# The values' projection of a sparse-attention layer moved behind compression and gates, with the first scores between its units

## The reference, cut to what matters

```python
q, k_c, v_c, k_s, v_s, k_w, v_w, gate = jnp.split(h @ w_in, split_at, axis=-1)   # 1024, 6 x 256, 48
gate = jax.nn.sigmoid(gate)
blocks = kv(t)[:, cidx] + pe                # 31 overlapping blocks of 32 tokens
kc = silu(blocks_k @ w1[0]) @ w2[0]         # compressed keys;  vc: the same of v_c
o_c = softmax(q kc^T - slope * dist) vc     # compressed branch
o_s = softmax(q k_s^T - slope * dist) v_s   # selected branch (here every block is selected)
o_w = softmax(q k_w^T - slope * dist) v_w   # window branch (the window holds all 512 tokens)
return (gate0 * o_c + gate1 * o_s + gate2 * o_w) @ w_out
```

## Time and profile before

| what | value |
|---|---|
| median of 3 runs | 2295.69 us (2295.18 to 2296.01) |
| profiled execution | 2294.17 us |
| its span, first to last instruction | 2292.9 us |
| TensorE busy | 2247.9 us, 98% of the span |
| VectorE, ScalarE, GpSimd busy | 72%, 46%, 28% |
| mean granted clock of TensorE | 0.998 |
| SyncE's queue, share of the 16 DMA engines | 30.3% |

### The profile page before, as it was taken

One profiled execution on the slowest core, in us unless ns is written; L12 is line 12 of the kernel. 1 busy time (PEld: TensorE's weight loads), 2 busy tenths in 40 slices (PEclk: granted clock), 3 DMA queues, 4 the chain that ended last, 5 costly groups with the idle time before them and its releaser, 6 DMA issues.

```text
span 2292.9 us, 34766 instructions
## 1 busy us (share of the span) xinstructions
PE 2247.9 (98%) x14151; PEld 1946.4 (85%) x14151; DVE 1641.1 (72%) x2120; ACT 1050.3 (46%) x1515; POOL 634.3 (28%) x557
## 2 busy tenths in 40 slices
PE   7999999999999999999999999999999999999999
PEld 5888778999887867778999888999887868899987
DVE  6668657889785456637888567989456984788844
ACT  4322534555334457734555346444345363544432
POOL 0110223332122048703332011332011870233200
PEclk9999999999999999999999999999999999999999
DMA  9654156775763210026774536775232202787322
GB/s 333 191 166 139 47 174 165 189 178 121 267 211 103 81 57 1 1 69 174 183 190 112 166 97 170 183 178 123 96 102 92 83 29 78 189 192 173 105 92 83
DMA packets 224373, 308.69 MB, mean 135 GB/s; under 512 B 14345, under 2 KB 165446, under 8 KB 223958
## 3 DMA queue, kind: packets, MB, share of 16 engines
q1 hardware_dynamic: 173268, 223.99, 30.3%
q0 software_dynamic: 50640, 82.29, 17.5%
q10 hardware_dynamic: 306, 0.19, 0.0%
HBM read 302.23 MB, written 4.19 MB: 134 GB/s over the span
## 4 chain that ended last, share of the span: by engine, by line
PE 84%; DVE 10%; ACT 2%; POOL 2%; issue 1%; DMA 1%; ACTq 0%; SPq 0%; DVEq 0%
PE ps L732 41%; PE ps L1180 10%; PE ps L1182 10%; PE ps L1181 10%; PE ps L879 4%; DVE w_lo L2315 2%; DVE dsa_mask L3116 1%; PE ps L1306 1%; POOL nsa_p L3487 1%; PE ps L1322 1%; DVE small L3114 1%; PE ps L928 1%; DVE h_lo L2412 1%; ACT w_hi L1631 1%; PE ps L1295 1%
## 5 line engine op out<-in xcount | busy, mean ns | idle before, releaser
L2315 DVE TENSOR_TENSOR w_lo<-w_raw,w_hi 128x1024 fp32r<-128x1024 f32 (+1 forms) x466 | 652.3, 1401 | 480.8 <-ACT w_hi L1631 479.1
L1631 ACT ACTIVATE w_hi<-w_raw 128x1024 fp32r<-128x1024 f32 (+1 forms) x472 | 495.7, 1051 | 996.7 <-PE ps L732 579.3
L1180 PE MATMUL ps<-feat_t,w_hi 128*128 128x256 f32 x1152 | 326.5, 283 | 3.1 <-DVE hid L2819 2.3
L1181 PE MATMUL ps<-feat_t,w_hi 128*128 128x256 f32 x1152 | 326.0, 283 | 0.0
L1182 PE MATMUL ps<-feat_t,w_lo 128*128 128x256 f32 x1152 | 326.0, 283 | 0.0
L3340 POOL TENSOR_TENSOR w_raw<-w_raw,w_raw 128x1024 f32<-128x1024 f32 x72 | 177.7, 2468 | 453.9 <-DVE w_lo L2315 453.9
L732 PE MATMUL ps<-h_hi,w_hi 128*128 128x512 f32 (+1 forms) x712 | 279.9, 393 | 4.8 <-DVE w_lo L2315 3.1
L732 PE MATMUL ps<-h_hi,w_lo 128*128 128x512 f32 (+1 forms) x712 | 277.2, 389 | 0.0
L732 PE MATMUL ps<-h_lo,w_hi 128*128 128x512 f32 (+1 forms) x712 | 277.2, 389 | 0.0
L1180 PE MATMUL ps<-h_hi,w_hi 128*128 128x256 f32 x864 | 244.9, 283 | 1.9 <-DVE w_lo L2315 1.9
L1181 PE MATMUL ps<-h_lo,w_hi 128*128 128x256 f32 x864 | 244.5, 283 | 0.0
(11 more groups left out here) (459 smaller groups left out, 4205.8 us busy)
## 6 DMA issues: line engine op xcount, KB each, us to landing
w_raw<-in_ffn_w_up SPq DMA_DIRECT2D x126, 512.0 KB, 6.5
w_raw<-in_ffn_w_down SPq DMA_DIRECT2D x176, 256.0 KB, 3.3
w_raw<-in_ffn_w_up POOLq DMA_DIRECT2D x72, 512.0 KB, 7.7
m_raw<-in_ada_w POOLq DMA_DIRECT2D x56, 512.0 KB, 4.8
w_raw<-in_ffn_w_gate SPq DMA_DIRECT2D x54, 512.0 KB, 5.8
w_raw<-in_hg_w_in SPq DMA_DIRECT2D x64, 256.0 KB, 3.2
w_raw<-in_ffn_w_up SPq DMA_DIRECT2D x48, 256.0 KB, 3.1
w_raw<-in_nsa_w_in SPq DMA_DIRECT2D x40, 256.0 KB, 2.9
```

The source lines that it names most:

```text
L1180: K.nc.tensor.matmul(out, hi[:, w], m_hi, start=opens and kt == f == 0, stop=False, skip_group_check=True)
L1181: K.nc.tensor.matmul(out, hi[:, w], m_lo, start=False, stop=False, skip_group_check=True)
L1631: K.nc.scalar.activation(K.half(K.hi(u), width), K.half(K.raw(u), width), ACT.Copy) \
L2315: K.nc.vector.tensor_tensor(K.half(K.lo(u), width), K.half(K.raw(u), width), hi, ALU.subtract) \
```

## The change

The values' projection (group 4) comes last. Its loads and units are listed behind the gates'. TensorE's order becomes: groups 0, 1, 2, 3; both parts of `hidden` (now in bank 0); the four gate units (now in bank 2); then a wait for the last evacuation of group 3, since the values now go to banks 4 to 7; then the four units of the values with other work between them. ScalarE and VectorE keep group 3's evacuations one by one between the splits, now the splits of the gate units and of the first two value units. The calls of `tensor_stay_busy` in the mix go, except those in other stages. The wait for all of `key_twice` becomes one per unit. `kc` moves to another place in SBUF.

```diff
-        for gi, pieces in enumerate((... k_tiles(w, slice(512, 1024)), strided(0), strided(256), k_tiles(w, slice(2560, 2608)))):
+        for gi, pieces in (... (3, strided(0)), (5, k_tiles(w, slice(2560, 2608))), (4, strided(256))):
@@ tensor_nsa_in
-            nsa_evac(K, pe, 3)
+            nsa_evac(K, pe, 2)
-    for gi in range(5):
+    for gi in range(4):
...
+    for u in range(2):
+        hidden(u)
     u0 = K.unit["nsa", 5]
-    nsa_evac(K, pe, 3)
     for u in range(4):
         pe.wait_ge(*K["w_low"].at(u0 + u))
         tensor_unit_products(K, None, u0 + u, gate_items(K, (u0 + u, u)))
-        if u < 2:
-            hidden(u)
+    nsa_evac(K, pe, 3)
+FIRST_UNITS = 3
@@ tensor_nsa_mix
-    nsa_evac(K, pe, 2)
-    nsa_evac(K, pe, 4)
-    pe.wait_ge(*K["key_twice"].at((3, 1, 1)))
-    for n in range(UNITS + 3):
+    u0 = K.unit["nsa", 4]
+    def values_in(u):
+        pe.wait_ge(*K["w_low"].at(u0 + u))
+        items = token_items(K, (u0 + u, u), range(4, 8), 512, by_bank=u == 3)
+        tensor_unit_products(K, ("nsa_in", "v"), u0 + u, items, (lambda n: None) if u == 3 else None)
+    values_in(0)
+    turn_gates()
+    pe.wait_ge(*K["c_hidden_out"].at(0))
+    scores(0)
+    values_in(1)
+    compressed_keys()
+    scores(1)
+    values_in(2)
+    scores(2)
+    values_in(3)
+    for n in range(2, UNITS + 3):
...
+        if FIRST_UNITS <= n < UNITS:
+            scores(n)
+        if n == 2:
+            nsa_evac(K, pe, 4)
+            compressed(0, 0)
...
-        if n == 0:
-            tensor_stay_busy(K, 4, 6)
-            turn_gates()
-        if n == 2:
-            tensor_stay_busy(K, 1, 4)
...
-        elif n == 4 or n == 5:
-            kept(n - 3, 4)
-            tensor_stay_busy(K, 3 if n == 4 else 2, 4)
...
+        if n == 2:
+            compressed(0, 1)
@@ scalar_nsa_in (vector_nsa_in in the same way)
-    for gi in range(6):
+    for gi in (0, 1, 2, 3, 5):
         u0 = K.unit["nsa", gi]
         for u in range(4):
-            if 0 < gi < 5:
-                evac(gi - 1, u)
+            if gi:
+                evac(3 if gi == 5 else gi - 1, u)
             scalar_split(K, u0 + u + 2)
+            if (gi, u) == (5, 1):
+                act.wait_ge(*K["c_hidden_bias"].at(0))
+                nc.scalar.activation(K.c_sig[:, :, 0:31], ..., ACT.Sigmoid, ...).then_inc(*K["c_gate"].up(0))
@@ scalar_nsa_mix
+    scalar_split(K, u0 + 2)
+    gates()
+    for n in range(FIRST_UNITS):
+        for t in (3, 2, 0, 1):
+            weights(n, t)
+        if n < 2:
+            scalar_split(K, u0 + n + 3)
+        if n == 0: ...
+    value_tile(0)
+    value_tile(2)
+    scalar_split(K, u0 + 5)
+    compressed(0, 0)
+    for n in range(FIRST_UNITS, UNITS + 4):
@@ vector_nsa_in
+            if (gi, u) == (5, 0): ...
+            elif (gi, u) == (5, 2): ...
@@ vector_nsa_mix
+    vector_split(K, u0 + 2)
+    for n in range(FIRST_UNITS):
+        for t in (3, 2, 0, 1):
+            scores(n, t)
+        reciprocal(n)
+        if n < 2:
+            vector_split(K, u0 + n + 3)
+        if n == 0:
+            for j in range(4):
+                compressed_value(j)
+    value_tile(1)
+    value_tile(3)
+    vector_split(K, u0 + 5)
+    for n in range(2, UNITS + 4):
```

More of the change, by code:

```diff
@@ L1286, in tensor_nsa_mix, with scores @@
     nc, pe = K.nc, K.pe
-    def scores(u, slot):
+    def scores(u):
         i, head, br = unit_of(u)
[L1290 to L1297, removed]
+        at = i + 4 * br
+        pe.wait_ge(*K["key_twice"].at((at // 2, at % 2, 1)))
+        for slot in range(3):
+            if u:
+                pe.wait_ge(*K["nsa_max"].at((u - 1, SLOTS[slot][-1])))
+            for t in SLOTS[slot]:
+                w, tok = (t + 1) * P, slice(t * P, (t + 1) * P)
+                out = K.ps[:, score_bank(t), IN_SLOT[t]:IN_SLOT[t] + w]
+                nc.tensor.matmul(out, K.nq[:, head, tok], K.nk[:, at, 0:w], start=True, stop=False)
+                nc.tensor.matmul(out, K.nq[:, head, tok], K.nk_lo[:, at, 0:w], start=False, stop=True) \
+                    .then_inc(*K["nsa_scores"].up((u, t)))
     def turn(u, bank):
@@ L1344, in compressed_keys @@
         pe.wait_ge(*K["c_zero_vec"].at(0))
+        pe.wait_ge(*K["c_exp"].at("gates"))
         for rows in (slice(0, 64), slice(64, P)):
-            ins = nc.tensor.matmul(K.ps[rows, 6, 0:128], K.w2[0:64, :], hs[0:64, :, :], start=True, stop=True)
+            ins = nc.tensor.matmul(K.ps[rows, OUT_BANK, 0:128], K.w2[0:64, :], hs[0:64, :, :], start=True, stop=True)
         for j in range(4):
             for gr in range(4):
-                ins = nc.tensor.matmul(K.ps[32 * j:32 * j + 31, 6, 128 + gr * 64:192 + gr * 64], hs[64:P, gr, 0:31],
+                ins = nc.tensor.matmul(K.ps[32 * j:32 * j + 31, OUT_BANK, 128 + gr * 64:192 + gr * 64], hs[64:P, gr, 0:31],
                                        K.w2[64:P, :], start=True, stop=True)
@@ L1402, in tensor_nsa_mix @@
                 turn(n - 2, bank)
-        if n % 2 and n < UNITS:
+        if n == 2:
+            compressed(0, 1)
+        elif n % 2 and n < UNITS:
             compressed((n - 1) // 8, (n - 1) % 8)
@@ L2117, in keep, with value_tile @@
         keep_turned(u, 6)
-    for n in range(UNITS + 4):
+    def value_tile(t):
+        act.wait_ge(*K["feature_sum"].at((("nsa_in", "v"), t)))
+        nc.scalar.activation(K.nv[:, t, :], K.ps[:, 4 + t, :], ACT.Copy).then_inc(*K["act_evac"].up(("nsa", 4, t)))
+    u0 = K.unit["nsa", 4]
+    scalar_split(K, u0 + 2)
[6 more added lines that the diff above has]
+        if n == 0:
+            act.wait_ge(*K["c_value"].at(0))
+            nc.scalar.activation(K.kc[:, :, :], K.ps[:, OUT_BANK, 0:128].rearrange("p (a b) -> p a b", a=4), ACT.Copy) \
+                .then_inc(*K["c_key_high"].up(0))
+    value_tile(0)
[3 more added lines that the diff above has]
+    for n in range(FIRST_UNITS, UNITS + 4):
         if n >= 7 and n % 4 == 3:
@@ L2130, in scalar_nsa_mix @@
             keep(n - 2)
-        if 1 <= n < UNITS and (n - 1) % 8 == 5:
+        if n < UNITS and (n - 1) % 8 == 5:
             compressed((n - 1) // 8, 5)
@@ L2135, in scalar_nsa_mix @@
                 weights(n, t)
[L2136 to L2140, removed]
+        if n < UNITS and (n - 1) % 8 != 5:
             compressed((n - 1) // 8, (n - 1) % 8)
@@ L3069, in vector_nsa_mix @@
             keep_turned(n - 3)
-        if n < UNITS:
+        if FIRST_UNITS <= n < UNITS:
             scores(n, 3)
-        if 1 <= n <= UNITS:
+        if FIRST_UNITS < n <= UNITS:
             reciprocal(n - 1)
-        if n < UNITS:
+        if FIRST_UNITS <= n < UNITS:
             for t in (2, 0, 1):
                 scores(n, t)
[L3077 to L3081, removed]
+        if n < UNITS:
             compressed((n - 1) // 8, (n - 1) % 8)
```

74 lines of the change are left out of this document (31 added, 43 removed).

## The result

The changed kernel takes 2299.28 us (median of 16 runs, 2297.47 to 2302.77), the kernel before 2294.81 us (16 runs, 2291.65 to 2299.01) in the same comparison: a ratio of 1.0022, 95% interval 1.0016 to 1.0029. That is 4.5 us, 0.2%, slower, and the interval reaches from 3.7 to 6.7 us. The forecast was 4.3 us more.

The account below looks back on a forecast made before the run. GpSimd's chain was taken to bound the mix's start, TensorE what follows. The subtraction 2.6 us later plus 1.7 us of clock made +4.3 us on 2295.69, so 2300.0 us; range 2293.9 to 2302.5.

Parts of the forecast that it names:

- The one number to compute: Start of GpSimd's subtraction at the mix's start: 2.6 us later before the clock; the 11.2 us behind it stay the same.
- The gates' wait: In the gate units, TensorE waits 0.7 us for unit 3's split, which is late behind evacuations of group 3.
- The new wait: Ahead of the values, TensorE stands idle 4.3 us until the last bank of group 3 is evacuated.
- The clock: Behind the new idle stretch the clock falls, adding 1.7 us; bounds nothing and twice as much.
- rival (b): A second or longer fall of the clock, in the values or at the mix's start: 2301.7, up to 2302.5 us; chance 0.22.
- (a): The forecast itself, with one fall of the clock: 2300.0 us, 0.19% more; chance 0.40.
- The copy of the last values' bank: Ahead of the compressed scores, TensorE waits for VectorE's copy: 0.65 us and two hand-overs, listed as 1.0 us.
- The constants and idle stretches at the mix's start, taken at nothing: Removing 2.6 us of constants' matmuls gains nothing there; idle 1.9 and 1.4 us ahead of two scales cost nothing, 1.7 for the range.
- Rival (d): Group 3's banks are drained in time, so the idle 4.3 us and the clock's fall go: 2294.0 us; chance 0.13.
- Rival (e): GpSimd's chain does not set the mix's start's pace; with (d), -5.1 us: 2290.6 us, 0.22% faster; chance 0.06.
- The table load's cost: On ScalarE before the sigmoid: taken as 1.28 us; with the skill's drain 2.66 us, making the idle time 5.7 us.

Follow-up runs that it names:

- the fill: The changed kernel with nine matmuls of constants put into TensorE's idle stretch ahead of the values: 2296.04 us, ratio 1.0008 to the kernel before.
- Drain first: The changed kernel, but ScalarE and VectorE empty all four banks of group 3 ahead of gate unit 2's split: 2292.73 us, ratio 0.9993 to the kernel before.
- the constants back: The changed kernel with the stay-busy matmuls at n = 4 and n = 5 put back: 2299.68 us, ratio 1.0020 to the kernel before.
- all biases late: The changed kernel, but GpSimd makes all three later compressed biases behind scale 6 of each eight units: 2305.68 us, ratio 1.0043 to the kernel before.
- the two runs on the constants: Stay-busy matmuls at n = 4 and 5 put back in the changed kernel (ratio 1.0020), and taken out of the kernel before (1.0001).
- first bias late: The changed kernel, but GpSimd makes only the first later compressed bias behind scale 5: 2296.51 us, ratio 1.0012 to the kernel before.
- its two variants: The kernel before without constants at n = 4 and 5: 2294.85 us, 1.0001; the same with the first compressed bias behind scale 5: 2292.62 us, 0.9988.
- the kernel with the drain, `hidden` and the first bias changed: The changed kernel with group 3 emptied first, halves of `hidden` between gate units, first compressed bias behind scale 5: 2292.07 us, ratio 0.9991.
- the fastest one among them: The changed kernel with `hidden` interleaved, first compressed bias late, and group 3's banks emptied two, one, one between splits: 2289.30 us, ratio 0.9979.

## Why the prediction was right

The sum was +4.3 us and the range 2293.9 to 2302.5; measured were +4.5 us (16 runs) and +4.12 us between the marks of the two traces. Point by point:

- *The one number to compute.* That only the start of GpSimd's subtraction counts held: 11.23 us from there to unit 3's transposes in both kernels, and one bias less in GpSimd's chain shortened this to 8.9 and the whole by 0.1%. One reading of the kernel before was incomplete. VectorE's maximum ends there at 845.63, but GpSimd is busy with a scale until the subtraction starts at 845.75, so its own work held the subtraction as much as the maximum did; after the change it had been idle for 10.62 us and only the maximum released it. The row of the kernel before:

```profile
843.40 2.38 POOL L3487 TENSOR_SCALAR nsa_p<-nsa_p,nsa_stat,nsa_gate 128x512 f32<-128x512 f32 x4 [1.07 <-DVE nsa_stat L3023]
```

- *The gates' wait*: 0.7 forecast, 0.54 measured.
- *The new wait*: 4.3 forecast, 4.14 measured; the values started 19.25 us behind group 3 and not 19.8. The split behind the first gate unit began 0.2 us earlier than forecast, and from it to the end of the drain it took 8.9 us (806.39 to 815.31) and not 9.2. What came behind made up for it: from the values' start to the subtraction the forecast had 33.2 us at full clock, and the two kernels with the drain or the fill took 33.5. That these two errors cancel was luck. "Drain first" showed that this wait is the drain.
- *The clock*: +1.7 forecast. The fill isolates it at 1.62 us in the traced execution. The ground for the term was thin, one fall behind 2.01 us of idle time, and behind the same 2.01 us the clock held in the changed kernel's trace; behind the 4.1 us it fell in all four traces that have this stretch. The changed kernel's traced execution is the fastest of the sixteen (2297.47 us). The mean granted clock over the sixteen was 0.9962, over the 81 executions of the kernel before that were timed beside the experiments 0.9976; over 2296 us of span this is about 3.3 us, an estimate (each clock is recorded to 0.001). So in the usual execution the clock probably cost more than 1.7 us, and rival (b), a longer fall, was not told apart from (a): the traces with the constants back and with all biases late, which have the same idle stretch, show a longer one. The drain and the fill also gained more in the times (6.7 and 3.2 us by the ratios) than in the traces (4.9 and 1.6).
- *The copy of the last values' bank*: 0.7 in the forecast's timetable and 1.0 in its list of differences, 0.83 measured.
- *The constants and idle stretches at the mix's start, taken at nothing*: confirmed by putting them back and by taking them out, 1.0020 and 1.0001. The clock did not fall there in the traces without the constants, though the stretch of 1.8 us lies close to the 2.01 us of the earlier trace rows; rival (b)'s second fall was not seen in the changed kernel's trace.
- *Rival (d)*, the drain in time, was wrong for the changed kernel, and "drain first" is what it described: forecast 1.7 us faster than before, 0.8 us in the trace. Of the 0.9 us between, 0.5 lie ahead of the values (15.99 us instead of 15.5): the split of their first unit, which (d) had left uncounted, takes 1.58 us of waiting, and the wait in the gates and the earlier start give back some of it. The rest lies between the values and the subtraction.
- *Rival (e)* fell with the two runs on the constants.

The table load's cost, where a page of the Trainium skill ("ScalarE: Activation LUTs", "What ACT_TABLE_LOAD costs") counts a drain of 1.38 us more, is settled by the trace after: the split ahead of the load ends at 808.19, the load takes 1.28 us from 808.22, and the sigmoid starts at 809.51. This trace does not agree with the page's drain.

What stays open is what the clock costs in the usual execution. Only one execution of each kernel has a trace, and the times of one kernel spread over some 3 to 8 us.

## What to carry to other kernels

Before moving a stage behind another, list what the old order covered: here the long projection hid the emptying of four banks, and the short units that took its place could not. Emptying that stands in an engine's program between the splits of the next units runs at the pace of those splits, so it starts when the units do; write it ahead of them if the next user of the banks is near. Matmuls that do nothing, placed where TensorE waited for another engine, cost nothing here, and where the clock held without them their removal gave nothing; in the stretch of 4.1 us, behind which the clock fell, they gave 1.6 us back. So do not count their removal as a gain; shorten the other engine's chain instead, at a place where that engine is idle, and check one cycle later.

## What the runs showed of the hardware

One fall of the clock had no fixed price. Between the values' first matmul and the subtraction, the same work took 33.5 us in the kernels whose clock held (33.53 with the drain first, 33.56 with the fill), 35.18 and 35.17 in two with the fall (the changed kernel and the first bias late), and 35.96 and 36.02 in two more with the same idle stretch (all biases late, and the constants back): 1.6 to 2.5 us for an idle stretch of 4.1 us, behind which the clock fell in all four. The windows view of one of the two dearer ones, with the constants back at n = 4 and 5, whose values start at 819.27:

```profile
815.00:819.20 4.20, 0.15 (x1) 0.00 (x0) 4.11 (x6) 3.19 (x4) 3.66 (x5) 0.82 0.45 145
819.20:824.00 4.80, 4.73 (x11) 3.77 (x12) 1.92 (x3) 0.00 (x0) 4.12 (x6) 0.50 0.57 190
```

Here the clock had fallen already in the idle stretch (0.82), and it was 0.50 over the next 4.8 us, where the changed kernel had 1.00 and 0.62. Idle stretches of 1.9 us were followed by full clock in one kernel, and by half clock in another:

```profile
853.90:855.80 1.90, 0.07 (x2) 0.00 (x0) 1.90 (x10) 1.50 (x5) 1.90 (x5) 1.00 0.00 0
855.80:860.00 4.20, 2.83 (x20) 2.54 (x21) 3.28 (x14) 3.14 (x10) 4.20 (x7) 1.00 0.01 2
```

```profile
876.60:880.10 3.50, 3.45 (x18) 1.69 (x18) 0.69 (x1) 1.85 (x6) 2.37 (x4) 0.59 0.00 0
```

The first two rows are the kernel before without constants, idle ahead of 855.86; the last one is the stretch behind the 1.86 us wait in the run with all biases late. Over those 3.5 us a clock of 0.59 is 1.4 us of work less.

The plainest case is the idle stretch of 2.01 us near 1771 us. It stands in the traces of all twelve kernels (2.01 or 2.02 us, once 2.18), with the same matmuls around it. In six of them the matmuls went from 0.39 to 0.63 us, the length they have at half clock, within the next 1.5 us: the kernel before and its two variants, drain first, first bias late, and the kernel with the drain, `hidden` and the first bias changed. In the other six, the changed kernel and the fastest one among them, the clock stayed at 1.00 over the next 4 us. So an idle stretch near 2 us cost about 1.4 to 1.7 us (3.4 x 0.49 in the earlier trace rows) or nothing, and the trace of one execution can't tell which it will be in the next. The stretch of 1.40 us near 707 us was followed by a granted clock of 1.00 over the next 4 us in all twelve traces.
